# First stage of a hybrid decoder layer: the GpSimd work moved to ScalarE and VectorE, a quarter of the modulation sums made one-column matmuls on TensorE, the input normalised by a diagonal matmul

## The reference

```
c_act = silu(c)                                    # 2048 numbers
mod   = c_act @ w_ada + b_ada                      # w_ada: 2048 x 12288 float32, 100 MB
sh1, sc1, gt1, sh2, sc2, gt2 = split(mod, 6)
h     = rms_norm(x, g_pre_mix) * (1 + sc1) + sh1   # x: 512 x 2048
proj  = h @ w_in                                   # w_in: 2048 x 5128
... RG-LRU scan, forgetting attention, output projection, MLP of width 8192 (not touched)
```

## Time and profile before

| | us |
|---|---|
| median of 3 runs | 2265.05 (2264.48 to 2266.9) |
| the profiled execution's own time | 2267.88 |
| its span in the profile | 2265.8 |

### The profile page before, as it was taken

The page is one execution under the profiler, slowest core; times in us unless marked ns, Lnnn a source line. Parts: engine busy times, 40 slices in busy tenths (PEclk is TensorE's granted clock), DMA queues, the critical chain, the costliest instruction groups (busy, mean ns, idle before and its releaser), DMA issues.

```text
span 2265.8 us, 25175 instructions
## 1 busy us (share of the span) xinstructions
PE 2136.9 (94%) x9081; PEld 1699.5 (75%) x9081; DVE 1627.8 (72%) x1783; ACT 801.1 (35%) x1032; POOL 162.1 (7%) x145
## 2 busy tenths in 40 slices
PE   4779998999989998999999999999999999999996
PEld 3557776888767776787787787787787787787775
DVE  7998698766676665767767767767767767767756
ACT  4123622222444334433433433333333333333432
POOL 3441040000121001000000000000000000000000
PEclk7889999999999999999999999999999999999998
DMA  9875458875424563323323223223223223233342
GB/s 330 290 238 156 149 159 286 288 251 175 140 92 166 201 212 113 93 84 115 99 83 119 94 84 120 93 86 117 93 91 112 93 97 107 93 101 102 96 169 89
DMA packets 178462, 321.43 MB, mean 142 GB/s; under 512 B 12600, under 2 KB 47528, under 8 KB 176096
## 3 DMA queue, kind: packets, MB, share of 16 engines
q1 hardware_dynamic: 172576, 303.12, 41.0%
q0 software_dynamic: 3568, 16.95, 2.1%
q10 hardware_dynamic: 2256, 0.53, 0.1%
HBM read 312.15 MB, written 8.42 MB: 141 GB/s over the span
## 4 chain that ended last, share of the span: by engine, by line
PE 69%; DVE 18%; issue 7%; ACT 5%; DMA 1%; DVEq 0%; ACTq 0%
PE pair L739 9%; PE pair L741 9%; PE pair L740 9%; DVE acc L1277 7%; PE pair L763 7%; PE pair L764 7%; PE pair L765 7%; PE bank L464 3%; PE bank L466 3%; PE bank L454 3%; PE bank L465 3%; PE bank L455 3%; PE bank L456 3%; ACT w_hi L1120 2%; DVE op_lo L1571 1%
## 5 line engine op out<-in xcount | busy, mean ns | idle before, releaser
L1604 DVE TENSOR_TENSOR yg<-yg,pair 128x1024 f32<-128x1024 f32 x240 | 289.8, 1218 | 316.7 <-PE pair L765 316.7
L739 PE MATMUL pair<-h_hi,w_lo 128*128 128x512 f32 x1024 | 407.3, 398 | 10.2 <-issue 10.2
L741 PE MATMUL pair<-h_hi,w_hi 128*128 128x512 f32 x1024 | 406.5, 397 | 0.0
L740 PE MATMUL pair<-h_lo,w_hi 128*128 128x512 f32 x1024 | 406.1, 397 | 0.0
L763 PE MATMUL pair<-w_hi,op_lo 128*128 128x512 f32 x840 | 333.6, 397 | 3.7 <-DVE op_lo L1571 3.5
L764 PE MATMUL pair<-w_lo,op_hi 128*128 128x512 f32 x840 | 332.8, 396 | 0.0
L765 PE MATMUL pair<-w_hi,op_hi 128*128 128x512 f32 x840 | 331.8, 395 | 0.0
L739 PEld LDWEIGHTS pair<-h_hi,w_lo 128*128 128x128 f32 x1024 | 193.0, 188 | 57.5 <-issue 11.0
L454 PE MATMUL bank<-h_hi,w_lo 128*128 128x512 f32 x512 | 215.7, 421 | 21.2 <-POOL h_lo L1742 10.5
L741 PEld LDWEIGHTS pair<-h_hi,w_hi 128*128 128x128 f32 x1024 | 193.3, 189 | 47.3
L740 PEld LDWEIGHTS pair<-h_lo,w_hi 128*128 128x128 f32 x1024 | 193.5, 189 | 46.8 <-issue 0.2
(11 more groups left out here) (252 smaller groups left out, 2892.8 us busy)
## 6 DMA issues: line engine op xcount, KB each, us to landing
raw<-in_w_ada_dram SPq DMA_DIRECT2D x128, 512.0 KB, 4.6
w_raw<-in_w_ff_dram SPq DMA_DIRECT2D x128, 512.0 KB, 3.8
raw<-in_w_ff_dram SPq DMA_DIRECT2D x128, 512.0 KB, 4.5
raw<-in_w_in_dram SPq DMA_DIRECT2D x82, 512.0 KB, 4.8
gst<-in_w_ada_dram SPq DMA_DIRECT2D x64, 512.0 KB, 6.1
raw<-in_w_out_dram SPq DMA_DIRECT2D x32, 512.0 KB, 3.6
x_tok<-in_x_dram SPq DMA_DIRECT2D x4, 1024.0 KB, 8.7
xr<-in_x_dram POOLq DMA_DIRECT2D x4, 1024.0 KB, 7.1
```

The costliest lines, as they stand in the source:

```text
L739: pe.matmul(b, lo[:, cols], h_hi[:, kt, :], start=(kt == 0), stop=False)
L740: pe.matmul(b, hi[:, cols], h_lo[:, kt, :], start=False, stop=False)
L741: last = pe.matmul(b, hi[:, cols], h_hi[:, kt, :], start=False, stop=(kt == KT - 1))
L1604: dve.tensor_tensor(y, y, pairs[2 + (i + r) % 2][:, :, :], ALU.subtract if i == 6 else ALU.add).then_inc(product_read, 1)
```

## The change

- GpSimd does nothing in the eight rounds. VectorE makes the low part of the odd weight unit too (`lo_part(2j-1)`, between the second and the third quarter's sums of the round) and `h_lo` (`h_low`). ScalarE makes the full float32 `h` in place, right behind each `h_hi`.
- The first quarter (rows 0 to 3 of a partition) is no longer summed on VectorE. TensorE multiplies it: `first_rows(j)`, 4 column blocks x 4 rows = 16 float32 matmuls whose stationary operand is a 128x128 block of `gst[0]` and whose moving operand is the one column c_k. The buffer `gst[0]` is handed back by `gst_turned`. VectorE sums 12 rows in place of 16.
- `first_rows(j+1)` stands behind unit 2j on TensorE, and `column_job(j+1)` now behind unit 2j+1; before it stood behind unit 2j.
- `take_start(j)` waits in round j itself, right behind its own sums, and adds the two partial sums (4 small instructions in place of 2).
- The token tile is not scaled. VectorE makes a 128x128 diagonal matrix of the reciprocals (`xdiag`), and a float32 matmul of the tile's blocks with it turns and scales them at once, in place of the transposes.

```diff
     def lo_count(n):
-        return n // 2 + 1 if n < U_LAST else n - 7
+        return n + 1
...
             def start_quarter(j, q):
-                i = 4 * j + q
                 if q == 0:
                     load_init(j)
-                if i >= 4:
-                    sp.wait_ge(gst_used, i - 3)
+                if j:
+                    sp.wait_ge(gst_used, 3 * (j - 1) + q) if q else sp.wait_ge(gst_turned, j)
...
         @block.tensor
             def sums_ready(m):
                 if m < 8:
-                    pe.wait_ge(gst_used, 4 * (m + 1))
+                    pe.wait_ge(gst_used, 3 * (m + 1))
...
+            def first_rows(j):
+
+                pe.wait_ge(gst_in[0], 32 * (j + 1))
+                if j >= 2:
+                    pe.wait_ge(mod_read, j - 1)
+                for b in range(4):
+                    at = 8 * (j % 2) + 4 + b
+                    for k in range(4):
+                        last = pe.matmul(banks[7][:, at:at + 1], gst[0][:, k, b // 2, b % 2 * P:(b % 2 + 1) * P], cc[:, 2, k:k + 1],
+                                         start=(k == 0), stop=(k == 3))
+                last.then_inc(gst_turned, 1)
...
             for t in range(NT):
-                pe.wait_ge(x_scaled, t + 1)
+                pe.wait_ge(xdiag_ready, t + 1)
...
-                    last = pe.transpose(banks[4 * (t % 2) + kt // 4][:, kt % 4 * P:(kt % 4 + 1) * P],
-                                        x_tok[:, t, kt * P:(kt + 1) * P], ident[:, :])
+                    last = pe.matmul(banks[4 * (t % 2) + kt // 4][:, kt % 4 * P:(kt % 4 + 1) * P],
+                                     x_tok[:, t, kt * P:(kt + 1) * P], xdiag[:, t, :], start=(kt % 4 == 0), stop=(kt % 4 == 3))
...
             pe.wait_ge(vcol_ready, 1)
+            pe.wait_ge(c_ready, 1)
+            first_rows(0)
             column_job(0, banks[7])
...
                     if n == 2 * j and j + 1 < 8:
-                        pe.wait_ge(mod_read, j + 1)
-                        column_job(j + 1, banks[7])
+                        first_rows(j + 1)
+                if j + 1 < 8:
+                    if j:
+                        pe.wait_ge(mod_read, j)
+                    column_job(j + 1, banks[7])
...
         @block.scalar
             for j in range(8):
                 hi_part(2 * j)
-                hi_part(2 * j + 1)
                 act.wait_ge(mod_read, j + 1)
                 for kt in (2 * j, 2 * j + 1):
                     act.activation(h_hi[:, kt, :], xnT[:, kt, :], ACT.Identity, bias=S1[:, kt:kt + 1],
                                    scale=A1[:, kt:kt + 1]).then_inc(h_hi_ready, 1)
+                    act.wait_ge(h_hi_ready, kt + 1)
+                    act.activation(xnT[:, kt, :], xnT[:, kt, :], ACT.Identity, bias=S1[:, kt:kt + 1],
+                                   scale=A1[:, kt:kt + 1]).then_inc(h_sum, 1)
+                hi_part(2 * j + 1)
...
         @block.vector
             def take_start(j):
                 dve.wait_ge(acc_read, j + 1)
-                step(dve.scalar_tensor_tensor(A1[:, 2 * j:2 * j + 2], banks[7][:, 0:2], 1.0, col(G_PRE_MIX, 2 * j, 2), ALU.add, ALU.mult))
-                dve.tensor_copy(S1[:, 2 * j:2 * j + 2], banks[7][:, 2:4]).then_inc(mod_read, 1)
+                at = 8 * (j % 2)
+                step(dve.tensor_copy(mod[:, :], banks[7][:, at:at + 4]))
+                step(dve.tensor_tensor(mod[:, :], mod[:, :], banks[7][:, at + 4:at + 8], ALU.add))
+                step(dve.scalar_tensor_tensor(A1[:, 2 * j:2 * j + 2], mod[:, 0:2], 1.0, col(G_PRE_MIX, 2 * j, 2), ALU.add, ALU.mult))
+                dve.tensor_copy(S1[:, 2 * j:2 * j + 2], mod[:, 2:4]).then_inc(mod_read, 1)
+                dve.wait_ge(mod_read, j + 1)
...
-                dve.tensor_scalar(x_tok[:, t, :], x_tok[:, t, :], stat[:, XR + t:XR + t + 1], None, ALU.mult).then_inc(x_scaled, 1)
+                if t == 0:
+                    dve.wait_ge(const_ready, 1)
+                dve.tensor_scalar(xdiag[:, t, :], ident[:, :], stat[:, XR + t:XR + t + 1], None, ALU.mult).then_inc(xdiag_ready, 1)
             dve.wait_ge(const_ready, 4)
+            def h_low(kt):
+                dve.wait_ge(h_sum, kt + 1)
+                dve.tensor_tensor(h_lo[:, kt, :], xnT[:, kt, :], h_hi[:, kt, :].bitcast(F32), ALU.subtract).then_inc(h_lo_ready, 1)
+
             for j in range(8):
-                start_sums(j, 0)
+                start_sums(j, 1)
+                start_sums(j, 2)
                 if j:
-                    take_start(j - 1)
-                for q in range(1, 4):
-                    start_sums(j, q)
+                    lo_part(2 * j - 1)
+                start_sums(j, 3)
+                take_start(j)
                 lo_part(2 * j)
-            take_start(7)
+                h_low(2 * j)
+                h_low(2 * j + 1)
+            lo_part(2 * 8 - 1)
...
         @block.gpsimd
-            for j in range(8):
-                slot, _, s = unit(2 * j + 1)
-                pool.wait_ge(hi_ready, 2 * j + 2)
-                pool.tensor_tensor(w_lo[:, s], raw[:, slot], w_hi[:, s].bitcast(F32), ALU.subtract).then_inc(lo_pool, 1)
-                ... (h in full and h_lo for kt = 2j, 2j+1)
```

More of the change, by code:

```diff
@@ L210, in hybrid_layer @@
         vec_turned, vcol_ready = sem("vec_turned"), sem("vcol_ready")
+        c_ready = sem("c_ready")
         c_exp, dve_step, act_step, pool_step = (sem(n) for n in ("c_exp", "dve_step", "act_step", "pool_step"))
         lam_exp, kp_ready = sem("lam_exp"), sem("kp_ready")
-        x_ssq, x_std, x_scaled, xt_done, xt_copied = (sem(n) for n in ("x_ssq", "x_std", "x_scaled", "xt_done", "xt_copied"))
+        x_ssq, x_std, xdiag_ready, xt_done, xt_copied = (sem(n) for n in ("x_ssq", "x_std", "xdiag_ready", "xt_done", "xt_copied"))
         h_hi_ready, h_sum, h_lo_ready = (sem(n) for n in ("h_hi_ready", "h_sum", "h_lo_ready"))
@@ L440, in unit_ready @@
             def unit_ready(n):
[L441 to L444, removed]
+                pe.wait_ge(lo_ready, lo_count(n))
             def w_tile(slot, k, width=COLS):
@@ L482, in column_job @@
                     if m < 8:
-                        last = pe.matmul(bank[:, b:b + 1], block_, ones[:, 0:1], start=True, stop=True)
+                        at = 8 * (m % 2) + b
+                        last = pe.matmul(bank[:, at:at + 1], block_, ones[:, 0:1], start=True, stop=True)
                     else:
@@ L1264, in _ @@
             step(dve.reciprocal(cc[:, 1, :], cc[:, 1, :]))
-            step(dve.tensor_tensor(cc[:, 2, :], cc[:, 0, :], cc[:, 1, :], ALU.mult))
+            dve.tensor_tensor(cc[:, 2, :], cc[:, 0, :], cc[:, 1, :], ALU.mult).then_inc(c_ready, 1)
+            dve.wait_ge(c_ready, 1)
             def weigh_rows(m, k0, rows, used, count):
                 a = acc[:, m % 2, :]
+                k_first = 4 if m < 8 else 0
                 for r, row in enumerate(rows):
                     k = k0 + r
-                    if k == 0:
+                    if k == k_first:
                         dve.wait_ge(init_in, 32 * (m + 1) if m < 8 else 16 * (m + 9))
@@ L1276, in weigh_rows @@
                             dve.wait_ge(acc_read, m - 1)
-                    ins = dve.scalar_tensor_tensor(a, row, cc[:, 2, k:k + 1], a if k else acc_init[:, :], ALU.mult, ALU.add)
-                    if k == 0:
+                    ins = dve.scalar_tensor_tensor(a, row, cc[:, 2, k:k + 1], a if k > k_first else acc_init[:, :], ALU.mult, ALU.add)
+                    if k == k_first:
                         ins.then_inc(acc_first, 1)
@@ L1288, in start_sums @@
                 dve.wait_ge(gst_in[q], 32 * (j + 1))
-                weigh_rows(j, 4 * q, [gst[q][:, r].rearrange("p a b -> p (a b)") for r in range(4)], gst_used, 4 * j + q + 1)
+                weigh_rows(j, 4 * q, [gst[q][:, r].rearrange("p a b -> p (a b)") for r in range(4)], gst_used, 3 * j + q)
             def ada_unit(a):
@@ L1731, in _ @@
             pool.memset(wig[:, :, :], 0.0).then_inc(gw_zero, 1)
-            for j in range(8):
-                slot, _, s = unit(2 * j + 1)
-                pool.wait_ge(hi_ready, 2 * j + 2)
-                pool.tensor_tensor(w_lo[:, s], raw[:, slot], w_hi[:, s].bitcast(F32), ALU.subtract).then_inc(lo_pool, 1)
-                for kt in (2 * j, 2 * j + 1):
-                    pool.wait_ge(h_hi_ready, kt + 1)
-                    pool.tensor_scalar(xnT[:, kt, :], xnT[:, kt, :], A1[:, kt:kt + 1], S1[:, kt:kt + 1], ALU.mult,
-                                       ALU.add).then_inc(h_sum, 1)
-                    pool.wait_ge(h_sum, kt + 1)
-                    pool.tensor_tensor(h_lo[:, kt, :], xnT[:, kt, :], h_hi[:, kt, :].bitcast(F32), ALU.subtract).then_inc(h_lo_ready, 1)
             for ch in range(CT):
```

5 lines of the change are left out of this document (2 added, 3 removed).

## The result

| | median us | runs |
|---|---|---|
| before | 2265.74 | 4 (2264.48 to 2266.9) |
| changed | 2282.44 | 4 (2281.94 to 2283.91) |
| ratio | 1.0074 | 95% interval 1.0059 to 1.0088 |

The changed kernel is slower by 16.7 us. Its profiled execution took 2282.24 us (span 2280.5), 14.4 more than that of the kernel before.

A forecast was written before the change was run, and what follows sets the result against it. VectorE, held up beside GpSimd, was taken to set 18.64 us rounds; the changed TensorE loop was 17.9 + 3.2 = 21.1 us. 36.0 + 7 x 21.1 + 14.0 ends unit 15 14.1 us later: 2279 us, range 2260 to 2292.

The forecast's parts named there:

- one loop through all of TensorE's work: First-stage rounds: each round's column job follows the odd unit and the next even unit needs its result; 21.1 us a round.
- The loop at the full clock: TensorE's round without low-clock loss: hand-off, both units, `first_rows`, column job and hop sum to 17.9 us, against 18.64 before.
- VectorE's saving: VectorE's work in a round falls to 13.8 us against 18.64; saving beyond its wait for TensorE is worth nothing.
- The clock: TensorE drops to 1.2 GHz after two lulls a round, hand-off and `first_rows`; 1.6 us each, 3.2 us a round.
- kept up: Rival: one-column matmuls count as work and keep TensorE's clock high; rounds of 17.9 us, 2255 us; chance 0.10.
- low for most of the round: Rival: TensorE's clock returns too late to help either unit; rounds of 22.9 us, 2292 us and above; chance 0.14.
- a clock below 0.78: Sign of the forecast: the first stage's granted TensorE clock falls below the 0.78 of the kernel before.
- The one-column matmul: In `first_rows` on TensorE, each of 32 records costs 0.111 us at the full clock, 3.6 us a round.
- The prediction's rival: One-column matmuls cost the skill's 25 ns floor: `first_rows` 0.8 us, round 18.3 us, 2259 us; chance 0.02.
- The start: Up to round 0's scale and shift: diagonal matmuls, `first_rows(0)` and column job end at 36.0 us, against 39.54 before.
- The tail: From round 7's scale and shift to the end of unit 15: 14.0 us, one low-clock lull included.
- Later stages: Everything behind the first stage was taken as unchanged, so unit 15's 14.1 us delay carries to the end: 2282 profiled.

The follow-up runs named there:

- e4: The changed kernel with four float32 128x448 matmuls of zeros added on TensorE behind each column job; 2269.64 us.
- e1: The changed kernel with the column job moved back ahead of the odd unit, right behind `first_rows`; 2267.6 us.
- e9: e1 with SyncE issuing the loads of the quarters in the order 1, 2, 0, 3 from round 1 on; 2255.24 us.
- e8: The changed kernel with one matmul in place of sixteen in `first_rows` for rounds 1 to 7, those sums left out; 2259.8 us.
- e2: The kernel before with only GpSimd's work of the rounds moved to ScalarE and VectorE, sixteen sums and TensorE's order kept; 2248.08 us.
- e3: The changed kernel with the old start, token tile scaled on VectorE and transposed, in place of diagonal matmuls; 2283.02 us.
- e5: The changed kernel with all sixteen sums on VectorE and no `first_rows`, the column job still behind the odd unit; 2289.83 us.
- e6: The changed kernel with `first_rows` moved to the hand-off ahead of the even unit, and the odd unit's low part one quarter earlier on VectorE; 2273.81 us.
- e10: e2 with two of the sixteen rows multiplied on TensorE right ahead of the column job, VectorE summing 14; 2239.69 us.

## Why the prediction was right

The step that mattered, that the round becomes one loop through all of TensorE's work, held. Its terms, as means over seven rounds of the changed kernel (the starts of the even unit, of `first_rows` and of the column job, differenced):

| term | predicted | measured |
|---|---|---|
| scale and shift to the first matmul | 2.4 | 2.57 |
| even unit, with its low stretch | 5.7 + 1.6 | 7.49 |
| `first_rows` and odd unit, with its low stretch | 3.6 + 4.3 + 1.6 | 9.84 |
| column job, four small instructions, hop | 1.85 | 1.81 |
| round | 21.1 | 21.7 |

- **The loop at the full clock.** e4 shows it bare, at 17.86 us. A column job not at the end of the loop takes it apart (e1, e9), and `first_rows` alone is 4.0 us of it (e8).
- **VectorE's saving is not on the path.** Its round fell from 18.0 to 13.3 us busy and it waits 45.3 us for eight column jobs. That the saving is real, e2 shows, where it is kept on the path.
- **The clock** is the mis-sized term: two lulls were to cost 3.2 us; 7.49 - 5.7 and 9.84 - 7.9 make 3.7. Between six and twelve matmuls run low behind a lull, not always eight, and the ends of some `first_rows` ran low too (3.92 and 4.23 us against 3.63), which I had charged at 0. The rival "kept up" is out with it, and so is "low for most of the round". The sign that I gave for it, a clock below 0.78, was badly chosen: the rounds of the kernel before read 0.77 to 0.88 and those of the changed one 0.76 to 0.84, so they overlap. The low stretches at the places named are what shows it.
- **The one-column matmul** costs what its rows said: 32 records in 3.63 us at the full clock, 0.113 each. The floor of about 25 ns in the Trainium skill (TensorE: Matmul & The Clock Gate, Back-to-back issue gap) is not contradicted by that: it is a least spacing, and the same section says that its isolated gaps hold no budget for the weight load, which each of these records has. The prediction's rival read it as a cost, and that reading is out.
- **The start.** The path that I added up is the one that ends last in the changed kernel (diagonal matmuls, `first_rows(0)`, column job), and its sum was 1.0 us long: 34.97 for 36.0. But it does not say why the start is earlier than before. e3 and e5 put either part back and the signal stays at 34.8; the gain is GpSimd's absence and the earlier read of the column job. The statement of the Trainium skill (TensorE: Matmul & The Clock Gate, Part 4: PE-mode transpose) that the high clock does not engage for transposes is left open by this. In e3 48 transposes ran with the clock at 1.00, but after a wait of 2.07 us and 16 more transposes `first_rows(0)` ran at 0.50. In e4 and e6 it ran low behind the diagonal matmuls too, so the transposes need not be the cause.
- **The tail** was 14.2 us for 14.0, so unit 15 ended 17.4 us later, not 14.1.
- **Later stages.** The stage ended 17.4 us later and the profiled executions differ by 14.4, so that 2282.24 meets the forecast of 2282 for this execution by luck. The 3 us stand in one place: between the modulation sum that starts at 584.5 us of the kernel before and the one at 680.1, 95.6 us pass, and 92.6 in the changed kernel. This is not the change: the same stretch takes 92.6 us in e2, e8 and e10 and 95.6 or 95.7 in e1, e3 and e9. The granted clock was 0.91 from 640 to 660 us of the kernel before and 1.00 in the 17 us of the changed one that answer to them; why a kernel gets the one or the other stays open. The medians differ by 16.7, close to the 17.4. Against them 2279 is 3.4 low, by the rounds (7 x 0.6 = 4.2 too short) and the start (1.0 too long).
- **Not seen at all:** SyncE's wait for `first_rows`, 58.7 us. VectorE waited 4.7 us for these loads here, all in the first rounds, and what their order cost in e1 is 12.4 us.

## What to carry to other kernels

When work moves from a busy engine to another, draw the round as a loop of who waits for whom: the saving counts only while the results that close the loop are made beside other work, one round ahead. Move first what is stuck beside a neighbour (GpSimd's work here, 17.7 us) and measure it alone; then move the rest row by row until the next limit, here by the figures the DMA engines, is met. And ask of every buffer that gets a new last reader which queue waits for it, and what stands behind that wait.

## What the runs showed of the hardware

- A two-input VectorE instruction of 0.75 us took up to 2.95 us beside GpSimd's tensor instructions (the longest of the 120 sums before), and never over 0.754 us in the stage once these were gone (e2, the changed kernel).
- Matmuls of zeros can hold TensorE at 2.4 GHz: in e4 3.25 us of them in each hand-off gave six even units of 5.69 us, and the granted clock read 1.00 for 23 us in one stretch, `first_rows` included. In the changed kernel, with none, the head of every even unit ran at 1.2 GHz (7.1 to 8.1 us).
- The same work behind the same wait can get either level: 32 one-column records took 3.75 us in one round of e6 and 6.73 in the next, behind 0.92 us of idleness each time, and 3.73 to 6.28 us ahead of round 0 in seven kernels. What decides it these runs do not show.
